# Reordering TensorE's first work behind three layer norms of a two-block transformer kernel

## The reference

```python
# first block
x = layer_norm(ALPHA * x + gated_deltanet(x, ...), ln_g[0, 0], ln_b[0, 0])     # norm 0
x = layer_norm(ALPHA * x + swiglu(x, gate, up, down), ln_g[0, 1], ln_b[0, 1])  # norm 1
x = layer_norm(ALPHA * x + swa_sink_attention(x, ...), ln_g[1, 0], ln_b[1, 0]) # norm 2
x = layer_norm(ALPHA * x + moe_swiglu(x, ...), ln_g[1, 1], ln_b[1, 1])         # norm 3
# second block: two layers of rmsnorm, sparse attention, RG-LRU, gated sum; rmsnorm

def layer_norm(x, g, b):
    mu = mean(x); var = mean((x - mu) ** 2)
    return (x - mu) * rsqrt(var + 1e-5) * g + b
```

## Time and profile before

| | before |
|---|---|
| runs, us | 2189.16, 2188.90, 2185.33 (median 2188.9) |
| profiled execution, us | 2189.52 |
| its span, us | 2187.7 |
| mean granted TensorE clock | 0.991 |
| TensorE matmul busy | 2128.4 us, 97% |
| VectorE busy | 1738.0 us, 79% |
| ScalarE busy | 1488.3 us, 68% |
| DMA | 564.72 MB, mean 258 GB/s |

### The profile page before, as it was taken

The page is one execution under the profiler, slowest core; times in us unless marked ns, Lnnn a source line. Parts: engine busy times, 40 slices in busy tenths (PEclk is TensorE's granted clock), DMA queues, the critical chain, the costliest instruction groups (busy, mean ns, idle before and its releaser), DMA issues.

```text
span 2187.7 us, 35000 instructions
## 1 busy us (share of the span) xinstructions
PE 2128.4 (97%) x13871; PEld 1888.8 (86%) x13871; DVE 1738.0 (79%) x2156; ACT 1488.3 (68%) x1992; POOL 393.5 (18%) x353
## 2 busy tenths in 40 slices
PE   8999999999999999999999999989999999999998
PEld 7888999877888888888888888869898998899998
DVE  5756555878999999999999999975698665689675
ACT  5644444566887888888888888864587845477864
POOL 1511000001011000000000000000667500458610
PEclk9999999999999999999999999999999999999999
DMA  8225855429999999999999999966655465655552
GB/s 280 97 71 124 270 186 172 155 88 358 355 369 387 395 387 392 383 378 378 388 377 378 364 394 378 386 225 197 182 163 178 139 222 183 185 160 174 162 162 103
DMA packets 326883, 564.72 MB, mean 258 GB/s; under 512 B 19873, under 2 KB 160953, under 8 KB 326713
## 3 DMA queue, kind: packets, MB, share of 16 engines
q1 hardware_dynamic: 314560, 527.60, 68.7%
q0 software_dynamic: 11760, 34.76, 5.8%
q10 hardware_dynamic: 392, 0.05, 0.0%
HBM read 548.32 MB, written 14.02 MB: 257 GB/s over the span
## 4 chain that ended last, share of the span: by engine, by line
PE 84%; DVE 10%; ACT 4%; issue 1%; DMA 0%; SPq 0%; ACTq 0%; DVEq 0%
PE bank L928 26%; PE bank L930 25%; PE bank L929 25%; DVE parts L2683 3%; PE bank L934 2%; PE bank L1089 1%; ACT parts L1985 1%; PE bank L1907 1%; DVE work L3492 1%; PE bank L1867 0%; DVE work L3495 0%; ACT work L2601 0%; DVE work L3493 0%; PE bank L1888 0%; DMA raw<-in_a_w_in_dram 0%
## 5 line engine op out<-in xcount | busy, mean ns | idle before, releaser
L2683 DVE TENSOR_TENSOR parts<-raw,parts 128x1024 fp32r<-128x1024 f32 (+2 forms) x709 | 857.0, 1226 | 312.8 <-ACT parts L1985 287.7
L1985 ACT CAST parts<-raw 128x1024 fp32r<-128x1024 f32 (+2 forms) x711 | 731.4, 1036 | 405.8 <-PE bank L930 392.2
L928 PE MATMUL bank<-cols,parts 128*128 128x256 f32 x1680 | 489.5, 291 | 11.7 <-DVE work L3605 4.8
L929 PE MATMUL bank<-cols,parts 128*128 128x256 f32 x1680 | 478.6, 285 | 0.0
L930 PE MATMUL bank<-cols,parts 128*128 128x256 f32 x1680 | 478.4, 285 | 0.0
L2683 DVE TENSOR_TENSOR fast<-raw,fast 128x1024 fp32r<-128x1024 f32 x302 | 361.8, 1219 | 24.3 <-ACT fast L1985 7.0
L1985 ACT CAST fast<-raw 128x1024 fp32r<-128x1024 f32 x302 | 316.3, 1052 | 84.7 <-PE bank L930 77.4
L928 PEld LDWEIGHTS bank<-cols,parts 128*128 128x128 f32 x1680 | 324.4, 193 | 19.0 <-issue 10.5
L929 PEld LDWEIGHTS bank<-cols,parts 128*128 128x128 f32 x1680 | 324.7, 193 | 2.8 <-issue 1.9
L930 PEld LDWEIGHTS bank<-cols,parts 128*128 128x128 f32 x1680 | 324.7, 193 | 0.0
L928 PE MATMUL bank<-parts,cols 128*128 128x512 f32 x740 | 293.7, 397 | 4.5 <-DVE parts L2683 2.5
(11 more groups left out here) (443 smaller groups left out, 3393.6 us busy)
## 6 DMA issues: line engine op xcount, KB each, us to landing
raw<-in_moe_w_gate_dram SPq DMA_DIRECT2D x112, 1024.0 KB, 8.6
raw<-in_moe_w_up_dram SPq DMA_DIRECT2D x112, 1024.0 KB, 8.1
raw<-in_moe_w_down_dram SPq DMA_DIRECT2D x112, 1024.0 KB, 8.7
raw<-in_w_in_dram SPq DMA_DIRECT2D x76, 1024.0 KB, 5.4
raw<-in_a_w_in_dram SPq DMA_DIRECT2D x12, 1024.0 KB, 11.5
raw<-in_ffn_w_gate_dram SPq DMA_DIRECT2D x11, 1024.0 KB, 5.4
raw<-in_ffn_w_up_dram SPq DMA_DIRECT2D x11, 1024.0 KB, 5.5
raw<-in_ffn_w_down_dram SPq DMA_DIRECT2D x11, 1024.0 KB, 5.1
```

Of the source, the lines that this page charges most:

```text
L928: pe.matmul(o, l[0], r[0], start=start, stop=False)
L929: pe.matmul(o, l[0], r[1], start=False, stop=False)
L1985: a.copy(dst[0], src).then_inc(*up(o + "hi", x))
L2683: v.tensor_tensor(dst[1], src, dst[0].bitcast(F32), ALU.subtract).then_inc(*up(o + "lo", x))
```

## The change

- The shift is turned by a matmul in transpose mode.
- Behind norms 0 and 1 the two pieces are multiplied by parts (`two_by_parts`): all products high by high first, half by half of the columns; then, of the first piece, low by high and high by low; then, of the second, high by low and low by high. It waits for bank 4, for high columns and high weights, and for each low part only where it is used.
- A new event `first` comes from the last matmul of the second tile's first half; VectorE's first residual half of the second tile waits for it and no longer for the end of the product.
- ScalarE casts the first tile's columns before the first piece of `last`, and the others of `last` come behind the second tile's columns; in norm 2 all of `last` comes behind the second tile.
- In norm 0 VectorE splits gate 0, up 0, gate 1 in that order (gate 0, gate 1, up 0 before).

```diff
-    "pe_used": ("used", "half"),
+    "pe_used": ("used", "half", "first"),
@@ out_step, ffn_down, swa_out: (t, k, h) == (1, 7, 0); (1, m - 1, 0); (0, 7, 0)
+                if (t, k, h) == (1, 7, 0):
+                    k_.then_inc(*up("first", 0))
@@ norm_cols
-                        pe.matmul(bank[b][:, j * 128:(j + 1) * 128], gb[:, 1, cs], ident, start=j == 0, stop=False, skip_group_check=True)
+                        pe.matmul(bank[b][:, j * 128:(j + 1) * 128], gb[:, 1, cs], ident, start=j == 0, stop=False, is_transpose=True, skip_group_check=True)
@@ behind norm 0; behind norm 1 it takes the place of the loop at L1555
-        pe.wait_ge(*at("lo_x", 0, 1, 1))
+        def two_by_parts(n, b, x0, x1):
+
+            two = [(bank[b][:, q * T:(q + 1) * T], piece_view(W, x)[1], x) for q, x in enumerate((x0, x1))]
+            claim(b)
+            for g in range(2):
+                pe.wait_ge(*at("hi_x", n, 1, g))
+                for o, w, x in two:
+                    if g == 0:
+                        pe.wait_ge(*at("hi", x))
+                    for k in range(4 * g, 4 * g + 4):
+                        pe.matmul(o, w[0][:, k], XT[0][:, k], start=(x, k) == (x0, 0), stop=False, skip_group_check=True)
+            o, w, x = two[0]
+            pe.wait_ge(*at("lo", x))
+            for k in range(8):
+                pe.matmul(o, w[1][:, k], XT[0][:, k], start=False, stop=False, skip_group_check=True)
+            pe.wait_ge(*at("lo_x", n, 1, 1))
+            for k in range(8):
+                k_ = pe.matmul(o, w[0][:, k], XT[1][:, k], start=False, stop=k == 7, skip_group_check=True)
+            k_.then_inc(*up("used", x))
+            o, w, x = two[1]
+            for k in range(8):
+                pe.matmul(o, w[0][:, k], XT[1][:, k], start=False, stop=False, skip_group_check=True)
+            pe.wait_ge(*at("lo", x))
+            for k in range(8):
+                k_ = pe.matmul(o, w[1][:, k], XT[0][:, k], start=False, stop=k == 7, skip_group_check=True)
+            k_.then_inc(*up("used", x))
@@ ScalarE, residual_norm
-            for y in last[:1]:
-                hi(W, MAIN, y)
-            for t in TILES[n]:
+            for i, t in enumerate(TILES[n]):
...
-                for y in (last[1:2], last[2:])[t == TILES[n][1]]:
+                for y in ((), last)[i] if n == 2 else (last[:1], last[1:])[i]:
                     hi(W, MAIN, y)
@@ VectorE, residual_norm
+            if n == 0:
+                rest.sort(key=lambda y: y != T_gu[0][0] and y != T_gu[0][1])
...
-                v.wait_ge(*ends[i])
...
                 for h, cs in enumerate(halves_):
+                    v.wait_ge(*(at("first", n) if (i, h) == (1, 0) else ends[i]))
```

More of the change, by code:

```diff
@@ L1443, in step @@
                             gi == 0 and j == 0, last and j == m - 1)
+                    if last and (t, j, h) == (1, m - 1, 0):
+                        k.then_inc(*up("first", 1))
                 return k
@@ L1461, in tensor_program @@
                 b = 4 + nb % 4
-                for q in range(2):
+                if nb == 0:
+                    two_by_parts(0, b, *T_gu[0])
+                for q in range(2 if nb else 0):
                     x = T_gu[nb][q]
@@ L1552, in attend @@
                 yield
[L1555 to L1564, removed]
+        two_by_parts(1, 4, *T_sk)
         busy[4] = ("swa_k",)
@@ L1605, in swa_out @@
                 k_ = mm3(bank[b][:, :], sl(XT, ALL, k, slice(t * 128, (t + 1) * 128)), sl(w, ALL, 0, slice(512 * h, 512 * h + 512)), k == 0, k == 7)
+                if (t, k, h) == (0, 7, 0):
+                    k_.then_inc(*up("first", 2))
             return k_
```

## The result

The changed kernel takes a median of **2184.01 us** (15 runs, 2179.61 to 2185.15). The kernel before, 15 runs, takes 2188.9 us (2185.19 to 2190.98). The ratio is 0.9978, with a 95% interval of 0.9971 to 0.9984, so there is a gain, of 0.16% to 0.29%. The means are 2183.32 and 2188.28, so by them the change gives 5.0 us, by the medians 4.9. The profiled execution took 2183.07 us (span 2181.3) against 2189.52, which is 6.45 less.

What follows compares the result with a forecast made beforehand. TensorE was taken as the bound, with 84% of the span, idling behind norms 0 and 1 for VectorE's low columns. Terms -2.0 - 1.5 - 1.35 = -4.85, with the clock -6.35, from 2189.52 gave 2183.2 us, range 2180.5 to 2187.5.

Steps and rivals of the forecast that it cites:

- the third case: Rival: transposes don't hold the clock up, a fall also behind norm 0; -3.35 us in all, 2186.2 us, chance 0.11.
- Norm 0, -2.0: First product behind norm 0 starts at 197.78 against 199.79, decided by the claim of bank 4, which waits for `lo_x`.
- Norm 1, -1.5: Behind norm 1, ScalarE's order lets VectorE start `lo_x` earlier; TensorE starts at 394.42 against 395.95.
- Norm 2 up to the columns, -1.35: Behind norm 2, VectorE's `lo_x` of tile 0 starts at 487.29, before at 488.63.
- Norm 2 behind the columns: Two splits and the logits follow as VectorE's own chain, which moves as a whole: 490.87 for 492.22.
- The clock behind norm 1, -1.5: The 3.4 us at clock 0.52 behind norm 1 goes, as its gap is split in two; bounds 0 and -1.5 us.
- the fall stays: Rival: the low clock behind norm 1 remains despite two shorter gaps; -4.85 us, 2184.7 us, chance 0.26.
- The shift, 1.78 to 0.89 us a tile: On TensorE, 8 transposes a tile take half the time of the 16 records; bounds 0 and 1.78 us.
- The shift still takes two records: Rival: transposes save nothing in the shift; -3.85 us in all, 2185.7 us, chance 0.04.
- Transposes don't hold the clock up: Rival: transpose mode doesn't count as busy, 3.4 us of low clock behind norm 0 costs 1.5 us; 2186.2 us, chance 0.11.
- The lead is taken back: Rival: in the experts' stage loads are the limit, so the earlier start gains little; 2189 us, chance 0.08.
- Slower by a long low clock: Rival: low clock lasts 10.3 us behind norms 0 and 1 and into the experts; +7.45 us, 2197.0 us, chance 0.04.

Runs made afterwards that it cites:

- a_bank: Changed kernel with the first products behind norms 0 and 1 in bank 6 in place of bank 4, readers matched; 2182.64 us, ratio to before 0.9971.
- a_no_turn: Changed kernel with the shift multiplied as before, 16 records a tile and not 8; 2186.47 us, ratio to before 0.9992.
- a_no_first: Changed kernel with VectorE's second residual waiting for the end of the product again; 2183.1 us in one run.
- a_no_casts: Changed kernel with ScalarE's old order, a piece of weights cast ahead of the first tile's columns; 2188.39 us, ratio to before 0.9999.
- a_no_parts: Changed kernel without products by parts: TensorE waits for both halves' low columns, then multiplies piece after piece; 2186.09 us, ratio to before 0.9991.
- a_96_turns: Changed kernel with 96 more transposes of 128 x 128, read by nobody, ahead of the first product behind norm 0; 2194.4 us in one run.
- a_96_mults: Changed kernel with 48 more float32 products without transpose mode, read by nobody, ahead of the first product behind norm 0; 2189.59 us in one run.
- a_again: Changed kernel, unchanged, profiled once more; 2185.94 us in one run.
- a_no_sort: Changed kernel with norm 0's waiting pieces split in the old order (gate 0, gate 1, up 0); 2185.25 us in one run.
- b_turn_only: Kernel before with the transpose mode of the shift alone; 2191.7 us in one run.

## Why the prediction was right, and where it was not

The forecast was 2183.2, between 2180.5 and 2187.5; the median is 2184.01. The gain by the medians is 0.22% of 2188.9, but the interval of 0.16% to 0.29% has on either side the 0.2% that the forecast drew as the line between faster and same, so which of the two it is stays open.

The profiled execution, against which the sum was made, took 2183.07, and that this is within 0.2 us of the forecast is luck. Of the 6.45 us, the terms of the sum gave 2.13 + 1.59 + 0.59 + 1.45 = 5.8 where 6.35 was forecast. Drift (0.37) and a low clock that happened not to come at 434 (1.66) added 2.0 that no term had, and low clocks behind the experts took 1.4 back. By its own words (one and a half steps of 1.5 below the forecast, the third case and one step) the range would be 2181.0 to 2187.7; the median lies inside either.

- **Norm 0, -2.0: measured -2.13.** Moved by the 0.37 us of drift, the forecast puts P of tile 1 at 194.45, `lo_x` at 196.67 and the first product at 197.41; they stand at 194.37, 196.55 and 197.29. These forecast starts count from the chain's 191.25, where the timeline has the shift's first record at 191.09; by the timeline TensorE would be ready for P 0.08 us earlier than it starts, and waits for the diagonal. That is small. The term that was said to decide, `claim` of bank 4, is shown by a_bank: with another bank the stretch is 1.07 us shorter, while `lo_x` and the splits keep their distances from the shift.
- **Norm 1, -1.5: measured -1.59.** The transposes and `first` give nothing there (a_no_turn, a_no_first), as forecast. ScalarE's order gives 0.95 (a_no_casts). But the forecast named only that order, and without the division by parts the stretch is 0.60 longer, as a_no_parts shows. That was in the working (TensorE starts at the end of half 0) and not in the sentence.
- **Norm 2 up to the columns, -1.35: measured -1.36** (5.91 for 7.27).
- **Norm 2 behind the columns: the step that failed.** "From the logits on everything is VectorE's own chain, which moves as a whole" put the logits' copy at 490.87, which is 483.66 with the drift of 7.21; it stands at 484.40, and only 0.6 of the 1.35 us arrives. The clock falls 7.95 us after the start of the shift, and before it fell 11.4 after it, so the last ten of the router's small products now lie in the low clock (0.21 us a step for 0.11) and the copy waits 0.77 us for them. In a_no_parts the fall came later, 9.41 us after the start and behind those products. Its window over most of the router's products, and its timeline row of the logits' copy:

```profile
483.00:487.00 4.00, 3.92 (x35) 3.79 (x34) 4.00 (x5) 3.08 (x6) 0.00 (x0) 1.00 0.49 142
```

```profile
487.12 0.15 DVE L3156 COPY work<-bank 128x16 f32<-128x16 f32 x1
```

  There the clock is 1.00, the copy waits for nothing, and logits come 9.60 us after the shift's start, 1.45 sooner than before, where the forecast had 1.35. The other profiles agree. In a_96_turns, a_96_mults, the changed kernel, a_again, a_bank and a_no_sort the fall came 7.82, 7.93, 7.95, 8.08, 8.14 and 8.48 us after the shift's start, and the copy waited 0.90, 0.78, 0.77, 0.65, 0.63 and 0.32 us; in a_no_first it came at 11.13 and the copy waited for nothing. So the cost is measured and grows the earlier the fall comes. Why it comes at one place in one execution and later in another stays open.
- **The clock behind norm 1, -1.5: right in the profile, too large as a mean.** It was taken as certain, from one execution. With the old order and its gap of 2.08 us the fall came in two profiles of three, and in b_turn_only with 2.48; with the changed order in none of eight (among them a_again and a_bank). So the change does take it away, and what it is worth is 1.5 times how often it came, about 1 us if two of three is the rate. The rival "the fall stays" is refuted. The gaps that were left are near the forecast's: from step to step, as it counted, 0.83 and 1.13 us for 0.9 and 1.3 (the profile, which counts from the end of a record, gives 0.69 and 0.89). It left out the short one before P of the first tile. "Nothing in the trace lies between 1.40 us and 2.08" holds for the two norms and not for the trace, which could have warned that a fall isn't certain. Timeline of the kernel before at three other gaps, and its windows behind them:

```profile
441.12 0.71 PE L934 MATMUL bank<-work 128*128 128x128 f32 x4 [2.14 <-DVE work L3076]
...
1658.04 0.36 PE L928 MATMUL bank<-cols,parts 128*128 128x256 f32 x1 [2.42 <-DVE work L3605]
...
1831.15 0.50 PE L928 MATMUL bank<-parts,cols 128*128 128x512 f32 x1 [1.80 <-DVE parts L2683]
```

```profile
441.00:445.00 4.00, 3.01 (x22) 2.40 (x23) 3.41 (x8) 1.19 (x4) 0.19 (x1) 0.57 0.00 0
1658.00:1664.00 6.00, 5.96 (x50) 5.99 (x51) 5.93 (x7) 1.05 (x1) 5.82 (x5) 1.00 0.86 277
1831.00:1837.00 6.00, 5.85 (x34) 5.11 (x35) 3.35 (x5) 1.18 (x3) 0.00 (x0) 1.00 0.57 178
```

  A gap of 2.14 us was followed by a low clock, one of 2.42 and one of 1.80 were not.
- **The shift, 1.78 to 0.89 us a tile: right.** The next record starts 0.88 us later (190.72 to 191.60). That is the price that no row showed, taken from the earlier trace rows. "The shift still takes two records" is refuted by the count of 48. What the forecast said of that case was right too: it gave norm 0 a gain of 0.85, norm 1 1.5 and norm 2 nothing, and a_no_turn has 0.89, 1.57 and 0.21.
- **No drain between the groups of products: right.** The 48 products behind norm 0 take 5.85 us from the first to the record behind them (197.29 to 203.14), and took 5.86 in the old order (199.79 to 205.65).
- **The sort, nothing: right**, by a_no_sort. **`first`, 0.3 at norm 2: 0.42**, and 0.37 at norm 0.
- **Transposes don't hold the clock up**, the rival of the Trainium skill (TensorE: Matmul & The Clock Gate, Part 4: PE-mode transpose): refuted for float32 by a_96_turns, in one execution. The trace disagrees with that sentence; 10.3 us of transposes ran at 1.00.
- **The lead is taken back**: refuted. DMA share 1.02 and 379 GB/s stand beside a lead that stays 7.8 us for 952 us.
- **Slower by a long low clock**: not seen. Behind norms 0 and 1 a low clock lasted 3.4 us in every profile that had one, and none of the changed kernel's had.

By the stretches the local terms are worth 2.13 + 1.59 + 0.6 = 4.3, with a mean of 1 for the clock 5.3; the means of 15 runs differ by 5.0.

## What to carry to other kernels

When operands are ordered so that a product can start early, look at what else it waits for: here the bank it writes into took back a full 1.07 us at each of two norms, and another bank gave it back for nothing. Value a queue's order by which engine is late at that place: by the stretches, transposes that halve a step's time gave 0.22 us alone and 2.4 with the rest of the change. A stretch of low clock seen in one profile is worth its cost times how often it comes, so look at the other gaps of the same trace, and profile the kernel more than once, before such a term goes into a sum.

## What was not expected of the hardware

- Behind norms 0 and 1 the fall of the clock goes with the length of TensorE's gap before the first product. Gaps of 1.84 to 2.48 us were followed by a fall in 6 of 7 norms (2.08 three times, with one exception; 2.43 and 2.48; 1.84 twice). Gaps of at most 1.49 us were followed by none, in 5 norms with `mm3` and in all of the changed order. Elsewhere in the kernel gaps of this length are a matter of chance. All fourteen profiles have one of 2.14 or 2.15 us near 440 us (433 to 446), one of 2.34 to 2.50 near 1655 and one of 1.80 near 1829, and a low clock began in it or within 1.6 us behind it in 7, 8 and 4 of them.
- Two gaps of 0.69 and 0.89 us, 2.0 us of matmuls apart, did not do what one of 2.08 did in two profiles of three.
- A float32 product of 128x128 by 128x128 takes two records of 0.11 us, the transposition of the same block one.
- Low clock elsewhere comes and goes between executions of one kernel. The stretch at 441.6 of the kernel before, 6.8 us at 0.50, costs 1.7 us; it is missing at 434 in the changed kernel's profile and there again in a_bank's. The end time of a single profile of this kernel can't tell 2 us from nothing; its stretches can.
